# First block of a two-block transformer kernel: attention moved between the k-tiles of units 13 to 23, gate units among the first delta steps, half of the output projection in the scan

## The reference

```
h    = rms_norm(x)
proj = h @ w_in                      # 1024 x 3592
q, k, v = rope(q), rope(k), v        # 8 heads of 64
attn = sum over 3 dilated patterns of softmax(q k) v, weighted by their log-sums
dq, dk, dv = silu(causal_conv4(proj[delta part]))      # 4 heads of 128
beta = sigmoid(..); g = -exp(a_log) * softplus(..)
o    = gated_delta_rule(l2norm(dq), l2norm(dk), dv, beta, g)   # chunks of 64 tokens, a triangular
                                     # inverse per chunk, then a scan over the 8 chunks
mix  = concat(attn, rms_norm(o) * silu(z)) @ w_out     # 1024 x 1024
x    = x + rms_norm(mix)
x    = x + rms_norm(conv_glu_ffn(rms_norm(x)))         # 1024 -> 2 x 2816 -> 1024
```

## Time and profile before

| what | value |
|---|---|
| runs of the kernel | 3183.1, 3194.47, 3227.76 us, median 3194.47 |
| the profiled execution | 3200.39 us, its span 3198.5 us |
| PE busy | 3045.5 us (95%), 14168 matmuls |
| DVE, ACT, POOL busy | 1222.3, 1149.4, 1246.7 us |
| mean granted PE clock | 0.951 |

### The profile page before, as it was taken

How to read it: one execution, slowest core, us unless ns; L and a number is a source line. 1 busy time by engine, 2 the same in 40 slices (tenths; PEclk the granted TensorE clock), 3 DMA queues, 4 the chain that set the end, 5 groups by cost and what they waited for, 6 DMA issues and landing times.

```text
span 3198.5 us, 42232 instructions
## 1 busy us (share of the span) xinstructions
PE 3045.5 (95%) x14168; PEld 2416.2 (76%) x14168; DVE 1222.3 (38%) x2193; ACT 1149.4 (36%) x1892; POOL 1246.7 (39%) x626
## 2 busy tenths in 40 slices
PE   8989999999999899999999998999999998999997
PEld 6778777888877787878888756677878656677876
DVE  3555325553054453155520558330012567330012
ACT  3343234443233433344432322533232323543331
POOL 2332123555433310235554333245463342145563
PEclk9999879999999997799999989999999989999999
DMA  3220002222322100122233111022222111112222
GB/s 113 86 66 1 1 20 73 92 95 97 106 66 86 53 1 1 33 66 94 97 99 105 60 42 60 27 66 99 92 92 93 55 53 53 34 66 96 94 92 92
DMA packets 60818, 217.32 MB, mean 68 GB/s; under 512 B 6576, under 2 KB 6704, under 8 KB 60432
## 3 DMA queue, kind: packets, MB, share of 16 engines
q1 hardware_dynamic: 60368, 214.48, 20.2%
q0 software_dynamic: 320, 1.12, 0.1%
HBM read 213.48 MB, written 2.10 MB: 67 GB/s over the span
## 4 chain that ended last, share of the span: by engine, by line
PE 81%; DVE 8%; ACT 3%; POOL 3%; issue 3%; DVEq 1%; DMA 0%; ACTq 0%; POOLq 0%; SPq 0%
PE bank L1669 52%; PE bank L1946 4%; PE bank L1848 3%; PE bank L1870 2%; PE bank L1716 2%; PE bank L1694 2%; POOL wL L652 2%; PE bank L1859 2%; PE bank L1773 1%; DVE bias L1540 1%; PE bank L1833 1%; PE bank L1724 1%; ACT wH L810 1%; PE bank L1807 1%; PE bank L1835 1%
## 5 line engine op out<-in xcount | busy, mean ns | idle before, releaser
L652 POOL TENSOR_TENSOR wL<-raw,wH 128x1024 fp32r<-128x1024 f32 x380 | 921.7, 2425 | 1155.2 <-ACT wH L810 1155.0
L1669 PE MATMUL bank<-hH,wH 128*128 128x512 f32 x1936 | 797.8, 412 | 33.7 <-DVE mT L1493 9.2
L1669 PE MATMUL bank<-hL,wH 128*128 128x512 f32 x1936 | 761.4, 393 | 0.0
L1669 PE MATMUL bank<-hH,wL 128*128 128x512 f32 x1936 | 761.1, 393 | 0.0
L1669 PEld LDWEIGHTS bank<-hH,wH 128*128 128x128 f32 x1936 | 366.8, 189 | 182.9 <-issue 94.0
L810 ACT ACTIVATE wH<-raw 128x1024 fp32r<-128x1024 f32 x380 | 399.6, 1052 | 262.7 <-PE bank L1669 249.8
L1669 PEld LDWEIGHTS bank<-hH,wL 128*128 128x128 f32 x1936 | 368.1, 190 | 79.4 <-issue 10.6
L1669 PEld LDWEIGHTS bank<-hL,wH 128*128 128x128 f32 x1936 | 367.3, 190 | 79.1
L1669 PE MATMUL bank<-hidH,wH 128*128 128x512 f32 x864 | 338.0, 391 | 1.8 <-POOL wL L652 1.6
L1669 PE MATMUL bank<-hidH,wL 128*128 128x512 f32 x864 | 336.4, 389 | 0.0
L1669 PE MATMUL bank<-hidL,wH 128*128 128x512 f32 x864 | 336.2, 389 | 0.0
(11 more groups left out here) (309 smaller groups left out, 4032.2 us busy)
## 6 DMA issues: line engine op xcount, KB each, us to landing
raw<-w_dram SPq DMA_DIRECT2D x398, 512.0 KB, 3.3
x<-x_dram SPq DMA_DIRECT2D x4, 512.0 KB, 9.3
out_dram<-x SPq DMA_DIRECT2D x1, 2048.0 KB, 6.2
const<-const_dram SPq DMA_DIRECT2D x1, 1421.5 KB, 13.0
par_next<-par_dram POOLq DMA_DIRECT2D x5, 168.0 KB, 2.6
qkT<-pos_dram POOLq DMA_DIRECT2D x1, 256.0 KB, 7.0
const<-const_dram SPq DMA_DIRECT2D x1, 130.5 KB, 2.1
```

The costliest lines, as they stand in the source:

```text
L652: pool.tensor_tensor(wL[:, s, :], raw[:, s, :], wH[:, s, :].bitcast(F32), ALU.subtract).then_inc(w_lo.sem, 1)
L1669: mm = pe.matmul(ACC[bk][:, :], wt[:, s, c:c + P], rhs, start=first and k == 0 and j == 0, stop=last and k == tiles - 1 and j == 2)
```

## The change

- `ORDER` no longer holds slots 0 to 32. Slots 3(v-13) to 3(v-13)+2 run inside unit v, for v from 13 to 23: on PE behind its k-tiles 0, 3 and 6, on DVE and ACT between the convolution's steps of unit v-1.
- SiLU is computed as (tanh(x/2) + 1) x by ACT and DVE, and the factor of two is taken out in the norms and in `HB`, half of beta. The table of Ln and Exp is loaded after units 19 and 23, and the inverse norms of q are made after unit 19.
- Units 24 to 27 (`gate_step`) go into banks 3 and 4 and stand in `ORDER` as `z` steps around slots 33 and 34, `small` and the `pre` steps 0 to 3 of the first pair. The four attention pieces follow them, in one place (`pieces`).
- The output projection is cut in two halves over k (`half_step`, each 3 matmuls): 20 of the 32 steps of the attention half stand among scans 4 to 7, 8 replace the 14 small matmuls, 4 follow the sums of squares. The delta half follows, and DVE adds the halves (`add_half`). The step j=1 of the last scan is gone. SP loads the weights of halves as two half units in one.
- Unit 39 writes bank 7 (`FOURTH`) and doesn't wait for `acc_free`. In the second block `fourth_low` comes ahead of the first `piece_low`.
- PE starts with 30 small matmuls on a tile of ones that DVE fills, ahead of the wait for the constants.

```diff
+ATT_AT = {v: tuple(range(3 * (v - 13), 3 * (v - 13) + 3)) for v in range(13, 24)}
+HALVES_IN = 20
...
+    z = [[("z", h, k) for k in range(KD)] + [("zout", h, 0)] for h in range(HN)]
+    scans = [[("scan", c, j) for c in range(4 * pair, 4 * pair + 4) for j in range(3) if (c, j) != (NCH - 1, 1)]
+             for pair in range(2)]
+    out = z[0][0:3] + [("att", 33, 0)] + z[0][3:6] + [("att", 34, 0)] + z[0][6:] + [("l2", 0, 0), ("small", 0, 0)]
+    out += z[1] + [("pre", 0, 0)] + z[2][0:4] + [("pre", 0, 1)] + z[2][4:] + [("pre", 0, 2)] + z[3][0:4]
+    out += [("pre", 0, 3)] + z[3][4:] + [("pieces", 0, 0)]
+    out += [("pre", 0, k) for k in range(4, PRE)]
     for k in range(PRE):
-        second += [("pre", 1, k)] + scans[0][k - 1:k] * (1 <= k <= 12)
-    first = [("small", 0, 0)] + [("pre", 0, k) for k in range(PRE)]
-    return (spread(first, 0, ATT_SPLIT[0]) + spread(second, *ATT_SPLIT) + spread(scans[1], ATT_SPLIT[1], SLOTS))
+        out += [("pre", 1, k)] + scans[0][k - 1:k] * (1 <= k <= 12)
+    done = 0
+    for m, step in enumerate(scans[1]):
+        out.append(step)
+        upto = HALVES_IN * (m + 1) // len(scans[1])
+        for i in range(done, upto):
+            out.append(("half", i // 4, i % 4))
+            if i % 4 == 1 and i > 4:
+                out.append(("hout", i // 4 - 1, 0))
+        done = upto
+    return out + [("hout", HALVES_IN // 4 - 1, 0)]
...
+                def half_out(h):
+
+                    if h % 2:
+                        low_of(w, HALF_OF[0][0] + h // 2 + 2)
+
                 for kind, a, k in ORDER:
-                    if kind == "att" and a % 8 == 2 and a >= 10:
-                        f = (a - 10) // 8
-                        piece_low(w, N_ATT1 + f, f % 2, att_place(w, f, hL), att_place(w, f, hH), heads)
+                    if kind == "zout":
+                        low_of(w, 26 + a)
+                    if kind == "pieces":
+                        for f in range(4):
+                            piece_low(w, N_ATT1 + f, att_piece(0, f), att_place(w, f, hL), att_place(w, f, hH), heads)
+                    if kind == "hout":
+                        half_out(a)
...
                 third_low(w, 1)
-                piece_low(w, N_HID2, 0, hidL2[:, 0, :], hidH2[:, 0, :])
                 fourth_low(w, 1)
-                piece_low(w, N_HID2 + 1, 1, hidL2[:, 1, :], hidH2[:, 1, :])
+                piece_low(w, N_HID2, piece[:, 0, :], hidL2[:, 0, :], hidH2[:, 0, :])
+                piece_low(w, N_HID2 + 1, piece[:, 1, :], hidL2[:, 1, :], hidH2[:, 1, :])
...
+                for u in range(24):
+                    slots = ATT_AT.get(u + 1, ())
                     if u < 12:
                         turn_input(w, u, u // 2, u % 2, u % 2, HD ** -0.5 if u < 4 else 1.0)
+                        if u >= 2:
+                            next_high(w, u // 2, u % 2)
+                        if u == 2 and L == 0:
+                            rope_angles()
+                        if u == 6:
+                            gate_functions(w)
                             use_table(EXP)
+                        continue
+                    c = u - 12
+                    if c >= 2:
+                        act.wait_ge(dn_act.sem, dn_act.at(w, c - 1))
+                    act.wait_ge(acc_scaled.sem, acc_scaled.at(w, c + 1))
+                    act.activation(xconv(c), ACC[u % 2][:, :], ACT.Copy,
+                                   scale=prm(w, "dconv", 4 * c + 3, 4 * c + 4)).then_inc(conv_in.sem, 1)
+                    next_high(w, u // 2, u % 2)
+                    for n in slots[0:2]:
+                        attention(w, n)
+                    act.wait_ge(acc_free[u % 2].sem, acc_free[u % 2].at(w, u // 2 + 1))
+                    act.activation(tanh_of(c), xconv(c), ACT.Tanh, scale=0.5).then_inc(tanh_done.sem, 1)
+                    for n in slots[2:3]:
+                        attention(w, n)
+                    if c < 8:
+                        act.wait_ge(dn_act.sem, dn_act.at(w, c + 1))
+                        square(w, 8 + c, c % 2, (dq, dk)[c // 4][:, c % 4, :], 0.5)
+                    if u in (19, 23):
+                        i = (u - 19) // 4
+                        use_table("natural_log_exp_and_others")
+                        act.wait_ge(l2_copied.sem, l2_copied.at(w, 4 * i + 4))
+                        act.activation(l2_stat(i), l2_stat(i), ACT.Ln, bias=cst("eps"))
+                        act.drain()
+                        act.activation(l2_stat(i), l2_stat(i), ACT.Exp, bias=cst(("qscale", "kscale")[i]),
+                                       scale=-0.5).then_inc(l2_rstd.sem, 1)
+                        if i == 0:
+                            use_table(EXP)
...
+                    elif kind == "zout":
+                        high_of(w, 26 + a)
+                    elif kind == "pieces":
+                        act.wait_ge(unit_done.sem, unit_done.at(w, 28))
+                        for f in range(4):
+                            piece_high(w, N_ATT1 + f, att_piece(0, f), att_place(w, f, hH), heads)
+                    elif kind == "hout":
+                        first_half(w, a)
...
+                first_half(w, 5)
+                first_half(w, 6)
...
+            def silu(w, c):
+
+                dve.wait_ge(tanh_done.sem, tanh_done.at(w, c + 1))
+                dve.scalar_tensor_tensor((dq, dk, dv)[c // 4][:, c % 4, :], tanh_of(c), 1.0, xconv(c), ALU.add,
+                                         ALU.mult).then_inc(dn_act.sem, 1)
+
+            def normalise(w, i, h):
+
+                tile = (dq, dk)[i][:, h, :]
+                dve.wait_ge(l2_rstd.sem, l2_rstd.at(w, i + 1))
+                dve.tensor_tensor(tile, tile, l2_stat(i)[:, h, :, :].rearrange("p h c -> p (h c)"),
+                                  ALU.mult).then_inc(l2_done.sem, 1)
...
+                    for n in slots[0:1]:
+                        attention(w, n)
+                    convolve(w, u - 12)
+                    for n in slots[1:2]:
+                        attention(w, n)
+                    silu(w, u - 12)
+                    for n in slots[2:3]:
+                        attention(w, n)
+                    if u >= 20:
+                        normalise(w, 0, u - 20)
...
+            pe.wait_ge(warm_in, 1)
+            for _ in range(30):
+                pe.matmul(WARM[:, 0:P], eb[0][:, 0, :], eb[0][:, 0, :], start=True, stop=True)
...
+                    if k in after:
+                        attention(w, after[k])
...
+            def gate_step(w, h, k):
+
+                u = 24 + h
+                if k == 0:
+                    pe.wait_ge(w_lo.sem, w_lo.at(w, u + 1))
+                    pe.wait_ge(sc_read.sem, sc_read.at(w, 32))
+                    pe.wait_ge(acc_free[h % 2].sem, acc_free[h % 2].at(w, u // 2))
+                c, out = k * P, SC[h % 2]
+                pe.matmul(out[:, :], wH[:, u % 2, c:c + P], hH[:, k, :], start=k == 0, stop=False)
+                pe.matmul(out[:, :], wL[:, u % 2, c:c + P], hH[:, k, :], start=False, stop=False)
+                mm = pe.matmul(out[:, :], wH[:, u % 2, c:c + P], hL[:, k, :], start=False, stop=k == KD - 1)
+                if k == KD - 1:
+                    mm.then_inc(unit_done.sem, 1)
...
+                        unit(w, u // 2, u % 2, u % 2, u // 2, KD, h_hi, h_lo,
+                             after=dict(zip((0, 3, 6), ATT_AT.get(u, ()))))
...
+                for i in range(HALVES_IN, 28):
+                    half_step(w, i // 4, i % 4, 0)
                 start(w, EVENTS, EVENTS - 2, EVENTS - 1)
-                keep_warm(ACC[0], 14)
-                pe.wait_ge(piece_ready.sem, piece_ready.at(w, N_ATT1 + 4))
...
+                for i in range(28, 32):
+                    half_step(w, i // 4, i % 4, 0)
...
+                for h in range(KD):
+                    for k in range(4):
+                        half_step(w, h, k, 1)
+                output_sum(w, 0)
+                first_three(w, 18, (0, 1), (22, 22), 1)
+                unit(w, 19, 1, 1, 23, KD, h_hi, h_lo, out=FOURTH)
...
```

More of the change, by code:

```diff
@@ L533, in l2_stat, with att_piece @@
             return (kdec, qkT)[i][:, :, :, :]
-        DSTAT = bank[3:7]
+        DSTAT = (bank[5], bank[6], bank[2], bank[0])
+        def att_piece(b, f):
+            if b == 0 and f < 2:
+                return mb[f][:, :, :].rearrange("p h c -> p (h c)")
+            return piece[:, f % 2, :]
         def rope_r(b):
@@ L1034, in _ @@
                                 act.activation(dk[:, :, t * P:t * P + P], heads(DB[e % 3][:, :]), ACT.Copy).then_inc(free.sem, 1)
-                    elif k == 2:
+                    elif kind == "scan" and k == 0 and a == 4:
+                        use_table(SILU)
+                        for h in range(HN):
+                            act.wait_ge(acc_free[h % 2].sem, acc_free[h % 2].at(w, 13 + h // 2))
+                            act.activation(zT[:, h, :], zT[:, h, :], ACT.Silu).then_inc(z_ready.sem, 1)
```

(13 more changed lines are left out.)

290 lines of the change are left out of this document (134 added, 156 removed).

## The result

| | before | after |
|---|---|---|
| median | 3194.41 us (20 runs, 3179.69 to 3246.51) | 3180.62 us (20 runs, 3166.71 to 3194.17) |
| profiled execution | 3200.39 us, span 3198.5 | 3177.61 us, span 3175.6 |
| mean granted clock | 0.951 | 0.962 |

The ratio is 0.9937, 95% interval 0.9912 to 0.9962: the change gained 14 us where 58 were forecast. The time lies 0.6 us above the upper end of the range. "Within 2%" was the likeliest class, and it came so; but the size was wrong.

A forecast was written before the change was run, and what follows sets the result against it. PE, busy 95% of the span, bounds the kernel through its work, waits and low clock. 3200.4 - 17 (first layer) - 24 (second) - 14.5 (start) - 6.6 (second block) = 3138, taken as 3136 us; range 3095 to 3180.

The forecast's parts named there:

- units 13 to 23: First layer: 67 us before plus 55 for slots 0 to 32 and 5 for waits, sum 127 us.
- unit 24 to `pre` 5: First layer: 32.3 us of PE work, waits of 2, 5 and 7, and 4 for cold matmuls: 50.3, no gain.
- `pre` 5 to 22, first pair: 45.2 us before, less 9.1 for slots, 0.7 for a copy and 2.4 of low clock: 33 us.
- second pair, scans 0 to 3: 81.2 us before, less 11.4 for seven slots: 70 us, with the pauses from DVE's chain staying.
- scans 4 to 7: 73 us before, at clock 0.50; 19 of scan work and 13.8 of half steps at full clock: 34 us.
- feed-forward part: Unit 39 no longer waits for bank 1, unit 40 waits for ACT's weights, unit 41 gains 1 us: -1.
- (a): Slot 34's transpose waits for slot 33's scaled result, queued on ACT behind unit 23's Ln and Exp: PE waits 5 us.
- (b): `pre` 5 waits for its mask, queued on POOL behind unit 29's `wL` and four pieces: PE waits 7 us.
- The wait behind unit 19: ACT's two table loads, Ln and Exp there take 6.6 us and delay its queue: PE waits about 3 us.
- rival D: Scans 4 to 7 stay at the low clock and take 64 us: 3196 us, no change; chance 0.11.
- Rival E: Slots lower the clock in units 18 to 23, as transposes don't count as busy: +75 us a layer, 3286; chance 0.05.
- Rival B: Waits (a), (b) and the one behind unit 19 mostly covered, nothing cold behind: 12 us a layer less, 3112; chance 0.22.

The follow-up runs named there:

- experiment 8: Changed kernel with 16 of the 20 attention-half steps taken out of scans 4 to 7 and run behind them: 3209.71 us, ratio 1.0017.
- experiment 15: experiment 4 run again, on the chip of experiment 16: 3140.69 us, ratio 0.9779 to the kernel before.
- experiment 16: The changed kernel run again with no edit, on the chip of experiment 15: 3178.76 us, ratio 0.9928 to the kernel before.
- experiment 4: Changed kernel with slot 33 earlier on ACT, attention pieces split around `pre` step 4, and unit 29's narrowing behind `pre` step 5: 3139.7 us, ratio 0.9813.
- 14: experiment 4 plus ten half steps put in the `pre` steps' pauses and half steps 24 to 31 behind the delta pieces' spreads: 3123.37 us, ratio 0.9724.
- experiment 3: Kernel before with two more 128-column float32 matmuls in each slot from 20 on: 3211.32 us, ratio 1.0036.
- experiment 1: Kernel before with only the 30 small warm-up matmuls added at the start: 3192.9 us, ratio 0.9962.
- 2: Kernel before with only the second block's `fourth_low` put ahead of its first `piece_low`: 3212.66 us, ratio 1.0031.
- 7: experiment 4 with ten half steps taken from scans 4 to 7 into the `pre` steps' pauses: 3144.23 us, ratio 0.9812.
- 11: experiment 4 with half steps 24 to 31 moved behind the spreads of the delta pieces: 3136.18 us, ratio 0.9834.

## Why the prediction was wrong

By its own steps, first layer:

| step | forecast | after |
|---|---|---|
| units 13 to 23 | 127 | 131.3 |
| unit 24 to `pre` 5 | 50.3 | 48.3 |
| `pre` 5 to 22, first pair | 33 | 38.1 |
| second pair, scans 0 to 3 | 70 | 74.7 |
| scans 4 to 7 | 34 | 34.2 |
| tail | 52.2 | 52.7 |
| feed-forward part | -1 | +2.1 |

**Right.** The start (12.3 us up to the third unit, 13.4 up to unit 13, for 14.5). Waits (a) and (b): 5.2 and 5.3 us for 5 and 7. The wait behind unit 19: 3.2 for 3. Scans 4 to 7: 34.2 for 34, with their clock up, so rival D didn't come, and experiment 8 shows that the half steps did it. The tail. Rival E didn't come: from 100 to 240 the clock is 0.99, with up to five transposes in a slot (four of probabilities and, in every second one, one of the result; the prediction counted four). By the Trainium skill, "TensorE: Matmul & The Clock Gate", Part 4 (PE-mode transpose), transposes don't count as PE-busy. The trace neither confirms nor refutes that, since matmuls of 512 columns stand between all slots; it is only against what E made of it.

**In part luck.** Unit 24 to `pre` 5 is 2 us under its forecast although a third wait there, of `pre` 4 on DVE, took 3.8 us where 2 were put. Beside its 14.3 us of waits it has 34.0, 1.7 over the 32.3 of full clock, where 4 were put for cold matmuls; those behind wait (b) fall into the next row.

**The step that failed** is the pricing of the two `pre` stretches: all slots were subtracted at their full price, 9.1 and 11.4 us, and 2.4 us of low clock with them, as if what is left would run without a pause and at 2.4 GHz. "PE itself sets the pace without slots too" holds for steps 5 to 18, from which the earlier trace rows come. Behind them PE waits for DVE. The timeline of before at step 20 of the first pair, where a slot's product (L1870) stands:

```profile
276.39 0.56 PE L1870 MATMUL bank<-v,pt 128*128 128x64 f32 x4
277.28 2.02 PE L1946 MATMUL bank<-eb,xtb 128*128 128x128 f32 x16 [0.33 <-DVE eb L1376]
```

and of after, there and at the stretch's start:

```profile
287.65 3.79 PE L2059 MATMUL bank<-xb,eb 128*128 128x128 f32 x16 [5.35 <-POOL eb L726]
291.23 2.93 PE L2059 MATMUL bank<-mb,xtb 128*128 128x128 f32 x16
294.00 1.95 PE L2059 MATMUL bank<-xtb,mb 128*128 128x128 f32 x16
...
320.31 3.56 PE L2059 MATMUL bank<-eb,xtb 128*128 128x128 f32 x16 [1.63 <-DVE eb L1462]
```

The pause at step 20 grew from 0.33 to 1.63 us, 1.3, and the 16 matmuls behind it took 3.56 us instead of 2.02, 1.5 more. The first two steps behind wait (b) took 1.8 and 1.0 us over the third's 1.95; the forecast had put the cold behind its waits into the stretch before. Sum 5.6, for the 5.1 that the first pair is over its forecast; 2.8 of it are thus in the wrong row, not missing from the sum. The pause alone doesn't make the matmuls behind it cold. In experiment 15 it is as long, and they run at full clock:

```profile
307.87 2.05 PE L2062 MATMUL bank<-eb,xtb 128*128 128x128 f32 x16 [1.63 <-DVE eb L1465]
```

In the second pair PE's waits are the same as before. Before, 282 to 370 us:

```profile
PE bank L1948 <- DVE xtb L1366: 2.4, 1, 2.4
PE bank L1946 <- DVE eb L1376: 1.6, 1, 1.6
PE bank L1964 <- DVE eb L1351: 1.5, 1, 1.5
```

After, 325 to 402 us:

```profile
PE bank L2061 <- DVE xtb L1452: 2.3, 1, 2.3
PE bank L2059 <- DVE eb L1462: 1.6, 1, 1.6
PE bank L2077 <- DVE eb L1437: 1.5, 1, 1.5
```

What is new is the clock in between:

```profile
354.64 3.68 PE L2059 MATMUL bank<-xtb,mb 128*128 128x128 f32 x16
...
377.78 3.05 PE L2059 MATMUL bank<-xtb,mb 128*128 128x128 f32 x16
380.63 2.62 PE L2059 MATMUL bank<-xb,eb 128*128 128x128 f32 x16
```

against 2.05, 2.05 and 1.95 at full clock, and a step of 2.96 for 1.95 at 345.97: 1.6 + 1.0 + 0.7 + 1.0 = 4.3 of the 4.7 us. So of the 9.8 us over the forecast some 8.6 are matmuls at the low clock and 1.3 is a pause laid bare. The second execution of the changed kernel (experiment 16) has all these steps cold again, within 0.1 us of the same times. Why the clock falls at them is open: ahead of the step at 354.64 PE was busy without a pause for 10 us. The experiments agree as far as they reach: the two waits of 5.2 and 5.3 us are worth 17 to 19 us a layer with what runs cold behind them (the mixers of 15 beside 16). In the first layer 13.8 of that lies between the first z step and `pre` 5 (37.3 us for 51.2), 10.1 of it waits; the first pair takes 35.2 us for 38.0 (but 38.2 in experiment 4's own profile), and 72.7 for 75.8 pass from there to the first half step. In experiment 15 the steps at 377 to 383 are back at 2.05 and 1.95, while the one at 354 is not (3.59). That covering the pauses themselves pays is shown only together with the tail (14 beside 15: 3.9 and 9.4 us in the mixers).

**Other terms.** Units 13 to 23: the nine matmuls at 204.55 took 3.70 instead of 2.1 us behind the wait, 1.6 us of low clock not in the sum; small waits were 1.9 us (2 in the sum); 2.6 us have no name. Feed-forward part: unit 39 no longer waits (4.6 us before), but unit 40 waits for its weights, so the wait went one unit on. Before:

```profile
PE bank L1669 <- DVE mT L1493: 4.6, 1, 4.6
```

After:

```profile
PE bank L1758 <- POOL wL L681: 4.4, 1, 4.4
```

The forecast named unit 40's wait and gave it no price. Second block: the feed-forward parts gained 4.3 and 4.7 us, more than the 3.3 forecast, but the mixers of that block, which the change hardly touches, were 1.7 and 5.2 us longer, and so 4.5 of the missing us lie there. Another execution of the same kernel (experiment 16) has them at 1.1 us less and 3.1 us more than before: what one and the same kernel varies by is as large, and these runs show no cost of the change there.

**The second layer** was put at 7 us above the first, "and should not be after". It wasn't (864.9 beside 864.6 us), but the first had not gained either.

The four stretches of the first table add up: 2.2 + 15.3 + 17.3 + 4.5 = 39 us missed of 62. Of the 15.3 in the first layer 9.8 are the `pre` steps; units (4.3) and feed-forward part (3.1) are over by 7.4, and unit 24 to `pre` 5 came out 2 better. Rival B, fewer pauses, is where the kernel goes once waits (a) and (b) are taken away (3140, experiments 4 and 15), not where the change itself went.

## What to carry to other kernels

When work that stands between the steps of a chain moves away, what is left doesn't run at the price of its busiest stretch: go through the steps one by one, and price each pause once bare and once with the matmuls behind it at half the clock, since both occur for the same pause (2.05 and 3.56 us for 16 matmul records here). Look for such a row in the trace of before (the earlier trace rows had one). And compare stages of profiles, not only medians, where an untouched stage moves by 15 us. When cover is moved to another stage, first list who stands in each queue at the place that it leaves; here moving one slot in ACT's queue, and two pieces and one narrowing of weights in POOL's, gave 38 us, more than the whole change.

## What the runs showed of the hardware

- A PE that is busy throughout can be at 1.2 GHz: 0.50 in before from 400 to 410 us. With the same instructions one layer's scans had 0.62, busy for 80.00 of 80 us, and the next one's 0.97, busy for 67.64 of 70 (experiment 3).
- 20 half steps of three 512-column matmuls among four scans went with a clock of 1.00; without 16 of them it was 0.50, and the same 518 matmul records were busy for 115.2 us instead of 95.3 (experiments 8 and 16).
- A warm-up of PE from 1 us on brings 12 us in most executions, but not in all (12 of 15 profiles), and neither pauses of 1.07 nor of 2.62 us before the first real matmul decide it. With 14 more warm-up matmuls the medians were 18 us higher (3158.19 beside 3139.7 and 3140.69), with a low-clock stretch 850 us later in both profiles. That the 14 matmuls are the cause isn't shown: the same stretch was cold in experiment 1, with 30.
- Gains of a few us from removed waits often don't show alone (experiments 1, 2, 7, 11), and then do together (14): whether a stretch is at 1.2 or 2.4 GHz moves more than the wait.
- The second block, with the same instructions, took 1410 to 1425 us in 14 profiles.
